# A 32-row spread for four tokens, interleaved top-16 searches and more places for key tiles in the last stage of a two-block model

## The reference

```python
def peer_ffn(x, w_q, sub_k1, sub_k2, u_tab, v_tab):
    ...
    v1, i1 = lax.top_k(s1, PEER_TOPK)
    v2, i2 = lax.top_k(s2, PEER_TOPK)
    cand_s = (v1[..., :, None] + v2[..., None, :]).reshape(bsz, seq, PEER_HEADS, PEER_TOPK * PEER_TOPK)
    ...
    top_s, pos = lax.top_k(cand_s, PEER_TOPK)
    experts = jnp.take_along_axis(cand_i, pos, axis=-1)
    gates = jax.nn.softmax(top_s, axis=-1)
    ...
        u = u_tab[ec].astype(f32)
        act = jax.nn.gelu(jnp.einsum('ced,cd->ce', u, xc.astype(f32))) * gc
        return jnp.einsum('ce,ced->cd', act, v_tab[ec].astype(f32)).astype(x.dtype)
```

## Time and profile before

| | us |
|---|---|
| median of 3 runs | 1909.29 |
| lowest and highest run | 1907.05, 1912.16 |
| the profiled execution | 1907.06 |
| its span | 1905.2 |
| PE busy in it | 1770.6 (93%) |
| DVE busy | 923.0 (48%) |
| ACT busy, POOL busy | 434.0, 427.1 |
| moved by DMA | 620.29 MB |

### The profile page before, as it was taken

How to read it: one execution, slowest core, us unless ns; L and a number is a source line. 1 busy time by engine, 2 the same in 40 slices (tenths; PEclk the granted TensorE clock), 3 DMA queues, 4 the chain that set the end, 5 groups by cost and what they waited for, 6 DMA issues and landing times. The chain is left out here.

```text
span 1905.2 us, 23747 instructions
## 1 busy us (share of the span) xinstructions
PE 1770.6 (93%) x9356; PEld 1135.2 (60%) x9356; DVE 923.0 (48%) x1988; ACT 434.0 (23%) x847; POOL 427.1 (22%) x312
## 2 busy tenths in 40 slices
PE   4989999988999999998899999999899998998998
PEld 4975444436887754442586556998788883333333
DVE  4467311115467842111599743978677662221222
ACT  5462211114345321110340324311111100000001
POOL 5820000006667600000110004313122221111120
PEclk8999899999999989999899999999999999999999
DMA  9885899995567769999632335399899999999996
GB/s 394 354 323 211 324 429 429 430 430 207 194 246 291 269 254 426 429 429 429 254 118 99 126 123 202 127 362 416 348 400 415 415 415 403 415 415 388 416 408 259
DMA packets 95089, 620.29 MB, mean 326 GB/s; under 512 B 11520, under 2 KB 12032, under 8 KB 60672
## 3 DMA queue, kind: packets, MB, share of 16 engines
q1 hardware_dynamic: 75824, 482.88, 63.7%
q0 software_dynamic: 18432, 134.23, 17.1%
q10 hardware_dynamic: 720, 1.61, 0.2%
HBM read 617.63 MB, written 1.05 MB: 325 GB/s over the span
## 5 line engine op out<-in xcount | busy, mean ns | idle before, releaser
L3110 PE MATMUL bank<-peer_tiles_a,peer_H 128*128 128x512 f32 x344 | 160.8, 605 | 19.0 <-DMA peer_tiles_a<-in_peer_v 18.9
L227 POOL TENSOR_TENSOR w_lo<-ring,w_hi 128x1024 fp32r<-128x1024 f32 x60 | 148.4, 2475 | 62.9 <-ACT w_hi L217 62.5
L3303 DVE CUSTOM_DVE_ANT_0 peer_junk<-peer_rows_b,bank 128x1024 bf16<-128x1024 f32 x64 | 76.7, 1217 | 138.5 <-issue 135.6
L3059 PE MATMUL bank<-peer_xT,peer_tiles_a 128*128 128x128 f32 x1120 | 136.8, 278 | 6.4 <-DMA peer_tiles_a<-in_peer_u 6.4
L3059 PEld LDWEIGHTS bank<-peer_xT,peer_tiles_a 128*128 128x128 f32 x1120 | 129.0, 192 | 21.3 <-issue 13.6
L1091 PE MATMUL bank<-ring,moe_slots 128*64 128x512 f32 x576 | 129.8, 601 | 9.5 <-DMA ring<-in_stream 9.5
L3110 PEld LDWEIGHTS bank<-peer_tiles_a,peer_H 128*128 128x128 f32 x344 | 61.7, 189 | 107.8 <-issue 65.7
L3303 DVE CUSTOM_DVE_ANT_0 peer_junk<-peer_rows_a,bank 128x1024 bf16<-128x1024 f32 x48 | 57.6, 1219 | 129.6 <-issue 119.3
L3172 POOL DMA_INDIRECT peer_rows_a<-in_peer_uv,peer_index x48 | 45.3, 944 | 293.5 <-PE bank L3090 242.5
L3172 POOL DMA_INDIRECT peer_rows_b<-in_peer_uv,peer_index x64 | 60.1, 939 | 212.5 <-PE bank L3090 197.6
L1272 DVE TENSOR_TENSOR bank<-bank,mod 128x512 f32<-128x512 f32 x32 | 22.4, 700 | 175.5 <-PE bank L1141 175.5
(11 more groups left out here) (520 smaller groups left out, 3724.1 us busy)
## 6 DMA issues: line engine op xcount, KB each, us to landing
ring<-in_stream SPq DMA_DIRECT2D x103, 2048.0 KB, 12.9
early<-in_stream SPq DMA_DIRECT2D x32, 2048.0 KB, 18.2
peer_tiles_a<-in_peer_v SPq DMA_DIRECT2D x86, 512.0 KB, 11.7
peer_tiles_a<-in_peer_u SPq DMA_DIRECT2D x70, 512.0 KB, 10.5
sb_mod_ring<-in_ada_t SPq DMA_DIRECT2D x64, 512.0 KB, 6.5
peer_tiles_b<-in_peer_v SPq DMA_DIRECT2D x42, 512.0 KB, 11.7
peer_tiles_b<-in_peer_u SPq DMA_DIRECT2D x34, 512.0 KB, 11.9
ret_mod_ring<-in_ada_t SPq DMA_DIRECT2D x32, 512.0 KB, 5.1
```

What stands on the lines that cost most here:

```text
L227: pool.tensor_tensor(self.shaped(self.w_lo, q, by_columns), self.quarter(n, q, by_columns), self.shaped(self.w_hi, q, by_columns).bitcast( ...
L3059: last = pe.matmul(K.bank[:, 2 + n // 4 % 2, n % 4 * P:(n % 4 + 1) * P], u[:, k, :], xT[:, k, :], start=(k == 0), stop=(k == KD - 1))
L3110: last = pe.matmul(K.bank[:, 2 + dh, :], H[:, m, :], first.slot(n)[:, dh * 512:(dh + 1) * 512], start=(m == 0), stop=(m == PK - 1))
L3303: dve.tensor_tensor_reduce(out=junk[:, i % 2, :], in0=rows[i % ROWS_HELD][:, 0:D], in1=wide_row(i % 2), scale=1.0, scalar=0.0, op0=ALU.mul ...
```

## The change

Seven edits, all in the last stage:

1. `spread_half` takes the place of `spread_pair`: four tokens at once, each by a product over 32 rows, and 512 of the 1024 columns. Token g of a quad has rows 32g to 32g+31 and bank 4+g. Two halves make a quad; the products are again eight.
2. `half_dots` takes the place of two `dot`: four operations of 512 columns, one for each token of the quad, and a half of the sum for each into `pre[:, q, half, g]`.
3. `open_quad` adds the two halves as the bias of the gelu, four operations of one column where there was one of four.
4. `picks` interleaves three chains: the two searches of head h and the search of the candidates of head h-1, step by step, each waiting only for its own former step (`Chain.behind`). The casts of eight heads become one, in `recover`. A half of dots stands behind each head.
5. `EARLY` is 48 instead of 64: the turned picks of the dense half and the gate units come 16 tiles sooner. The loop has ten rounds instead of eight; its last two have no gate units. `BESIDE_PICKS` is 16 instead of 20, so 76 tokens are done beside the key tiles (before: 68) and 52 among the value tiles (before: 60).
6. `FIRST_TILES` is 12 instead of 16, `FIRST_TOKEN` 18 instead of 23, `PICKED_AT` 39 instead of 59: the first picks are turned behind tile 11, and the first spread stands behind tile 19.
7. `SPARE` is 13 instead of 8 (places in `H` from row 64 on, and rows 16 and 32 to 63), used twice instead of up to tile 41; `READY_BEHIND` issues 17 tiles early instead of 12.

```diff
-FIRST_TILES = 16
+FIRST_TILES = 12
-EARLY = 64
-FIRST_TOKEN = 23
-SPARE = 8
+EARLY = 48
+FIRST_TOKEN = 18
+SPARE = 13
-BESIDE_PICKS = 20
+BESIDE_PICKS = 16
+READY_BEHIND = [0] * 6 + [1] * 4 + [2] * 3 + [4] * 4
...
+    def behind(self, running):
+
+        if self.n > running:
+            self.eng.wait_ge(self.sem, self.n - running)
...
-            for n in range(FETCHED, FETCHED + SPARE):
-                sp.wait_ge(K.chunk_used, n_wq + (1 if n < FETCHED + 4 else 2 if n < FETCHED + 7 else 4))
+            for n, chunks in enumerate(READY_BEHIND):
+                if chunks:
+                    sp.wait_ge(K.chunk_used, n_wq + chunks)
                 first.fetch(sp, n)
...
-                for dh in range(2):
-                    for n, part in enumerate(first.x_rows):
-                        for r in range(2):
-                            t, own = token(2 * p + r), slice(64 * r, 64 * (r + 1))
-                            last = pe.matmul(K.bank[:, 4 + 2 * r + dh, :], first.ident[own, t:t + 1].to_broadcast([64, P]),
-                                             part[own, dh * 512:(dh + 1) * 512], start=(n == 0), stop=(n == 1))
+                q, cols = p // 2, slice(p % 2 * 512, (p % 2 + 1) * 512)
+                for n, part in enumerate(first.x_rows):
+                    for g in range(QUAD):
+                        t, own = token(QUAD * q + g), slice(32 * g, 32 * (g + 1))
+                        last = pe.matmul(K.bank[:, 4 + g, :], first.ident[own, t:t + 1].to_broadcast([32, P]), part[own, cols],
+                                         start=(n == 0), stop=(n == 1))
...
-                act.activation(opened[:, q % 2, :], pre[:, q, :], ACT.Gelu_apprx_tanh).then_inc(quad_gelu, 1)
+                for g in range(QUAD):
+                    last = act.activation(opened[:, q % 2, g:g + 1], pre[:, q, 0, g:g + 1], ACT.Gelu_apprx_tanh, bias=pre[:, q, 1, g:g + 1])
...
+            def picks(tt, dots_behind):
+                for h in range(PK_HEADS + 1):
+                    scored, paired = h < PK_HEADS, h > 0
+                    others = 2 * scored + paired - 1
...
+                    for k in range(5):
+                        if scored:
+                            for half in range(2):
...
+                                c.behind(others)
+                                c.step(search_step(dve, k, val[:, h % 2, half, :], idx[:, half, h, :],
+                                                   scores[:, tt, m * PK:(m + 1) * PK]))
+                        if paired:
+                            c.behind(others)
+                            c.step(search_step(dve, k, best[:, h - 1, :], pos[:, h - 1, :], cand[:]))
```

More of the change, by code:

```diff
@@ L2876 @@
 TOKENS = P
[L2877 to L2883, removed]
+SPARE_ROWS = [64 + 8 * ((i + 1) % 8) for i in range(8)] + [16, 32, 40, 48, 56]
+FIRST_ROUND = [0, 1, 2, 3, 14, 15] + list(range(6, 14)) + [16, 17, 18, 4, 5]
+PLACE = FIRST_ROUND + [p for p in FIRST_ROUND if p != 14]
+FORMER, TURN = [], []
+while len(PLACE) < 2 * PK:
+    PLACE.append(min(range(SLOTS), key=lambda p: max(i for i, q in enumerate(PLACE) if q == p)))
+for _n, _p in enumerate(PLACE):
+    FORMER.append(max([i for i, q in enumerate(PLACE[:_n]) if q == _p], default=-1))
+    TURN.append(PLACE[:_n + 1].count(_p))
 SPARE_USED = max(i for i, p in enumerate(PLACE) if p >= SLOTS) + 1
+READY_BEHIND = [0] * 6 + [1] * 4 + [2] * 3 + [4] * 4
 class ExpertKeys:
@@ L2916, in __init__ @@
             sb("col", [P, 2, PK_HEADS]),
[L2917 to L2918 removed]
+            *floats,
         )
@@ L2943, in __init__, with search_step @@
             self.g_row = sb("gain_row", D)[:]
[L2946 to L2952, removed]
+def search_step(dve, k, values, index, src):
+    part = slice(0, 8) if k < 3 else slice(8, TOP)
+    if k == 2:
+        return dve.match_replace(src, values[:, part], src, TAKEN)
+    return dve.max_index(index[:, part], values[:, part], src) if k in (1, 4) else dve.max(values[:, part], src)
 def peer_stage(K, S, products, first, scores, room, out):
@@ L2998, in _ @@
             sp.dma_start(g_row, K.A["norm_f_g"].to_broadcast([P, D])).then_inc(gain_in, 16)
-            for n in range(FETCHED + SPARE, 2 * PK):
+            for n in range(len(READY_BEHIND), 2 * PK):
                 if FORMER[n] >= 0:
@@ L3289, in recover @@
                     c.do(dve.tensor_reduce(sel[:, half, tt, :], flat, AX.X, ALU.add))
+                    if half == 0:
+                        dots_behind(PK_HEADS + 1)
             def normalize(tt):
@@ L3339, in _ @@
             dve.tensor_tensor(first.x_rows[1][:], x_row, first.x_rows[0][:].bitcast(F32), ALU.subtract).then_inc(x_made, 1)
-            for h in range(PK_HEADS):
-                dve.wait_ge(s_taken, 2 * h + 1)
-                pick_head(1, h, lambda place: None)
-            recover(1)
+            picks(1, lambda h: None)
+            recover(1, lambda h: None)
             normalize(1)
@@ L3351, in _ @@
             dve.wait_ge(s_taken, 16)
-            for h in range(PK_HEADS):
-                pick_head(0, h, dot_at)
-            recover(0)
+            picks(0, half_behind)
+            recover(0, half_behind)
             normalize(0)
```

164 lines of the change are left out of this document (81 added, 83 removed).

## The result

The change makes the kernel slower by a third of a per cent: 1914.12 us (median of 14 runs, 1908.12 to 1916.7) against 1906.89 (14 runs of the kernel before, 1902.21 to 1912.16). The ratio is 1.0033, 95% interval 1.0022 to 1.0044. The forecast was 1899 with a range of 1886 to 1912: it has the wrong sign, and the range misses. The profiled execution took 1915.19 us, its span 1913.4.

What follows compares the result with a forecast made beforehand. DMA (634 us) was taken as the longer of two nearly equal loads, PE needing 618. Gains of 7.6 us at the loop's start and 2.5 behind it, together 10, took 1909.3 to 1899 us, range 1886 to 1912.

Steps and rivals of the forecast that it cites:

- The half spread: PE's spread of four tokens: 0.66 us for a half, saving 29 us of PE over 64 spreads.
- The rival of loads in a row: Spread: weight loads go one after another, a half takes 1.1 us, the kernel 1904 us; chance 0.08.
- The searches: Picks: interleaving cuts a head from 6.6 to 5.1 us; with earlier turned picks the index is ready at 1253.3.
- More places: Start of the stage: DMA is full from the start, and its first 7.7 us of shortfall shrink to about 1.
- The loop's start: Tile 48, where DVE, PE and DMA meet: first spread of the loop at 1335 us, a gain of 7.6 us.
- The rounds: Loop beside the key tiles: DMA keeps each of ten rounds at 25.3 us, while PE's round falls to 23.6.
- The prediction's own sign of being wrong: Gate units: PE waits for dots of 1 us and more would show the forecast wrong.
- this 0.5 us: Gate unit of a first half: PE's wait for the fourth row's half dot, from 1429.2 to 1429.7.
- the 1.7 us of PE's room: Loop: PE's slack in each round, taken to absorb the wait for the fourth row.
- The rival of the four rows for a half: Gate units: first-half dots need four rows, before two; 1.5 us at each of 19 quads, 28 us, 1927; chance 0.12.
- The value part: Among the value tiles: PE has a little more room, recovering 2 of DMA's 5.0 us shortfall.
- The sum: Whole kernel: 7.6 us at the loop's start and 2.5 us behind it, together 10 us less.

Runs made afterwards that it cites:

- e1: The changed kernel with spreads of two tokens, whole dots and one gelu for a quad put back, the rest of the change kept: 0.9981 of the kernel before.
- e2: The kernel before with only the spreads of four tokens, half dots and gelu by columns added: 1.0093 of the kernel before.
- e8: The kernel before with spreads of four tokens, half dots and gelu by columns only beside the value tiles: 1.0005 of the kernel before.
- e9: e1 with the first dot of each four tokens also waiting for the rows of the other three: 1.0138 of the kernel before.
- e3: The changed kernel with all but two pairs of gate units moved behind the second half of a quad: 0.9979 of the kernel before.

## Why the prediction was wrong

*The half spread.* Right: 0.67 us, forecast 0.66. The rival of loads in a row is refuted by the four loads of a half, together as long as one load of 128 columns:

```profile
1393.71 0.19 PEld L3082 LDWEIGHTS bank<-peer_x_rows_hi,peer_ident 32*128 32x128 f32 x4 [0.28 <-DVE peer_pre L3326]
```

By the rule of the Trainium skill ("TensorE: Matmul & The Clock Gate", section on LDWEIGHTS), P/1.2 ns for a load, four loads one after another would take 0.43 us, an estimate; in this trace loads to different rows don't go one after another, and the four lie within 0.19 us.

*The searches.* Right, a little better: a head takes 4.64 us, forecast 5.1.

```profile
1254.60 0.43 DVE L3287 TENSOR_TENSOR peer_cand<-peer_val 128x256 f32<-128x256 f32 x1
...
1259.24 0.42 DVE L3287 TENSOR_TENSOR peer_cand<-peer_val 128x256 f32<-128x256 f32 x1
```

The index was ready at 1251.9, forecast 1253.3.

*More places.* Mis-sized. DMA was to be full from 1230 on and short by about 1 us at the start. It moved 380 GB/s up to 1280 (355 before) and 373 from there to 1340 (416 before), 4.5 and 6.1 us short; in e1 380 and 383. So DMA was short less than before at first, and more behind it.

*The loop's start.* Forecast 1335, measured 1339.4 in the change and 1332.8 in e1. The chain DVE, PE and DMA was sized well. Of the 6.6 us between the two not much is sure to be the halves': the profiles of the same programs up to there are 1336.6 to 1339.4 with halves and 1332.8 to 1337.6 with pairs, on average 2.4 us apart. In e2, where the loop starts at 1381.2 and not at 1372.9 (e8: 1374.2), halves do cost beside the second picks, which I had taken at nothing.

*The rounds.* This is where it went wrong. Forecast 25.3 us, measured 26.4, which is 11 us over ten rounds. The prediction's own sign of being wrong, waits for dots at the gate units of 1 us and more, came true (eight, 1.2 to 4.0 us). **The step that failed is "In my forecast this 0.5 us vanishes in the 1.7 us of PE's room".** The rival of the four rows for a half had the right mechanism, place and sign, and was given 0.12. Three things in that step were mis-sized. The rival put the rows 1.65 us apart and the fourth 16.3 us behind the first gather (1412.70 to 1429.0). In the trace it lands 14.5 us after its own gather (1368.33 to 1382.8) and 18.2 us behind the first, and 18.0 to 19.9 us in the ten quads of the loop where DVE waits for it. The dots of the third and fourth row start 3.8 us apart, here (1379.04 and 1382.81) and in the quad of the longest wait:

```profile
1433.45 0.69 DVE L3326 CUSTOM_DVE_ANT_0 peer_junk<-peer_rows_b,bank 128x512 bf16<-128x512 f32 x1 [2.31 <-DMA peer_rows_b<-in_peer_uv,peer_index]
...
1437.23 0.69 DVE L3326 CUSTOM_DVE_ANT_0 peer_junk<-peer_rows_c,bank 128x512 bf16<-128x512 f32 x1 [3.08 <-DMA peer_rows_c<-in_peer_uv,peer_index]
```

The prediction's own figures could have warned of it: a row of 1.049 MB takes 2.5 us at 415 GB/s, and a row and a tile 3.8 us, an estimate. So in the loop the wait is 1.2 to 4.0 us, and not 0.5. The 1.7 us of room is an average over a round, while the wait falls on the first half of a quad, where PE comes sooner just because the spread became shorter. And three of the four waits of 2.75 us and more are followed by products at the lower clock, 1.4 to 1.6 us more each time. The rival's own 28 us was too much for the change: about 10 us, and 30 only in e9.

*The value part.* The forecast comes to 307 us (a span of 1895.2, less 1335 and ten rounds), measured 309.7; but that it is so near is luck. In e1, with the same number of tokens, it is 317.2. In e1's loop PE waits for key tiles:

```profile
PE bank L3064 <- DMA peer_tiles_a<-in_peer_u: 4.0, 3, 1.7
PE bank L3115 <- DMA peer_tiles_b<-in_peer_v: 2.1, 2, 1.5
PE bank L3064 <- DMA peer_tiles_b<-in_peer_u: 1.7, 2, 1.2
```

In the change it waits for none there, as its tiles lie ready. Six places hold 3.1 MB, 7.6 us at 415 GB/s, which fits the 7.5 us between the two value parts. That was not tested by itself. If it is so, the slow loop gave part of its loss back in the value part.

*The sum.* Forecast -10: 7.6 at the loop's start and 2.5 behind it, for PE's room. The shorter spread had a share in both: in the rival of loads in a row, where a half takes PE as long as a pair does, the sum came to 1904, which is -5. So edits 1 to 3 were good for about 5 us in my sum, and edits 4 to 7 for about 5. Measured, edits 4 to 7 gave -3.6 (e1), not far from it, and edits 1 to 3 cost +9.9. That makes +6.3, which is the measured 0.0033 (the two medians are 7.2 us apart). By the profiles of the change and of e1, edits 1 to 3 cost 13 us in the rounds and 6.6 at the start, and get back 7.5 in the value part.

Both e1 and e3 beat the kernel before and the change (0.9981 and 0.9979, intervals below 1). They are 3.6 and 4.1 us faster than before: less than the 0.3% of the prediction, but outside of their intervals.

## What to carry to other kernels

An edit that saves time on an engine that is not the bound is not free: ask which data each step needs that it didn't need before, and compare when the last of it lands with when the now faster engine arrives there, at that very step. Slack averaged over a round covers no wait that falls on one place of it. Where three engines meet at one handover, edits that each bring one of them forward must be costed together; one alone is given back.

## What the runs showed of the hardware

Of four waits of PE of 2.75 to 3.97 us in the loop three were followed by slower products (sixteen in 3.49, 3.33 and 3.50 us, otherwise 1.95), with a granted clock of 0.83 over 10 us behind the first; I hadn't expected that in a loop where PE is over 90% busy. The wait of 2.80 us at 1491.30 had no such effect (2.02 us), nor had the one of 1.16 us at 1409.44 (2.02 us), so the length of the wait alone doesn't decide it. Four weight loads of 32 rows each run side by side in the time of one, 0.19 us, and four products of 512 columns over 32 rows take 0.33 us together. A row fetch of one token took 14.5 us from issue to use beside full tile transfers, though the medians over the whole profile, from issue to landing, are 11.3 us for rows_b and 12.7 for rows_a. Third and fourth rows of a quad came into use 3.8 to 4.1 us apart in six quads of the loop.
